# An MLP's up product taken before its norm, and two more of its pairs in seven products

## The reference, cut to what matters

```python
x = x + (merged @ w_out[l]).astype(x.dtype)
h2 = rmsnorm(x, norm_mlp_g[l])               # x * rsqrt(mean(x*x) + 1e-6) * g
z = jnp.square(jax.nn.relu(h2 @ w_up[l]))    # w_up: 1024 x 4096
x = x + (z @ w_down[l]).astype(x.dtype)      # w_down: 4096 x 1024
return rmsnorm(x, final_norm_g)              # then the second block begins with its own norm
```

## Time and profile before

| | us |
|---|---|
| median of 3 runs | 1552.71 (1552.62 to 1553.04) |
| profiled execution | 1552.45 |
| its span | 1550.7 |
| TensorE busy | 1540.2 |
| VectorE busy | 1059.2 |
| ScalarE busy | 755.2 |

### The profile page before, as it was taken

The page is one execution under the profiler, slowest core; times in us unless marked ns, Lnnn a source line. Parts: engine busy times, 40 slices in busy tenths (PEclk is TensorE's granted clock), DMA queues, the critical chain, the costliest instruction groups (busy, mean ns, idle before and its releaser), DMA issues.

```text
span 1550.7 us, 22343 instructions
## 1 busy us (share of the span) xinstructions
PE 1540.2 (99%) x8348; PEld 1326.7 (86%) x8348; DVE 1059.2 (68%) x1759; ACT 755.2 (49%) x1305; POOL 71.6 (5%) x62
## 2 busy tenths in 40 slices
PE   9999999999999999999999999999999999999998
PEld 7877777788799999888888888888888899989987
DVE  6776887668789576357786545455555899948735
ACT  5445776654357445264444334344444545524514
POOL 0000000020000000040000010020002000000002
PEclk9999999999999999999999999999999999999999
DMA  5333223242323332223442232334123333322322
GB/s 194 122 109 99 85 75 96 95 136 82 123 95 103 103 96 92 99 96 119 129 131 67 75 129 90 112 120 159 59 82 109 109 103 109 123 96 82 108 90 75
DMA packets 56235, 161.88 MB, mean 104 GB/s; under 512 B 7232, under 2 KB 8640, under 8 KB 56000
## 3 DMA queue, kind: packets, MB, share of 16 engines
q1 hardware_dynamic: 55504, 159.41, 31.9%
q0 software_dynamic: 320, 0.52, 0.2%
q10 hardware_dynamic: 304, 0.52, 0.1%
HBM read 148.89 MB, written 2.10 MB: 97 GB/s over the span
## 4 chain that ended last, share of the span: by engine, by line
PE 95%; DVE 4%; ACT 0%; issue 0%; DMA 0%; DVEq 0%; SPq 0%; ACTq 0%
PE G L1440 64%; PE TP L1440 10%; PE SC L1440 9%; PE O L1440 5%; PE M L1440 5%; DVE WL L2551 1%; PE TP L1874 1%; PE TP L1820 1%; DVE MGl L2551 0%; DVE T L2910 0%; DVE T L2914 0%; DMA GN<-in_gains 0%; PE TP L1923 0%; DVE QK L2551 0%; DVE F L3172 0%
## 5 line engine op out<-in xcount | busy, mean ns | idle before, releaser
L1440 PE MATMUL G<-XGh,WH 128*128 128x512 f32 x920 | 363.7, 395 | 0.0
L2551 DVE TENSOR_TENSOR WL<-RAW,WH 128x1024 fp32r<-128x1024 f32 (+2 forms) x269 | 282.9, 1056 | 115.8 <-ACT WH L1961 115.4
L1440 PE MATMUL G<-XGh,WL 128*128 128x512 f32 x920 | 358.7, 390 | 0.0
L1440 PE MATMUL G<-XGl,WH 128*128 128x512 f32 x920 | 358.3, 389 | 0.0
L1961 ACT ACTIVATE WH<-RAW 128x1024 fp32r<-128x1024 f32 (+2 forms) x275 | 240.1, 881 | 111.0 <-PE G L1440 79.8
L1440 PEld LDWEIGHTS G<-XGh,WH 128*128 128x128 f32 x920 | 172.8, 188 | 38.6 <-issue 3.8
L1440 PEld LDWEIGHTS G<-XGh,WL 128*128 128x128 f32 x920 | 172.7, 188 | 36.9
L1440 PEld LDWEIGHTS G<-XGl,WH 128*128 128x128 f32 x920 | 172.9, 188 | 33.9
L1440 PE MATMUL G<-MGl,WH 128*128 128x512 f32 x372 | 144.9, 389 | 1.0 <-DVE MGl L2551 1.0
L2902 DVE TENSOR_TENSOR X<-X,G 128x512 f32<-128x512 f32 x75 | 51.4, 686 | 137.2 <-PE G L1440 137.1
L1440 PE MATMUL G<-MGh,WH 128*128 128x512 f32 x372 | 145.0, 390 | 0.0
(11 more groups left out here) (423 smaller groups left out, 3226.3 us busy)
## 6 DMA issues: line engine op xcount, KB each, us to landing
RAW<-in_dn SPq DMA_DIRECT2D x30, 512.0 KB, 3.3
RAW<-in_fg SPq DMA_DIRECT2D x22, 512.0 KB, 4.3
RAW<-in_up SPq DMA_DIRECT2D x20, 512.0 KB, 3.4
RAW<-in_g SPq DMA_DIRECT2D x16, 512.0 KB, 3.3
RAW<-in_f SPq DMA_DIRECT2D x14, 512.0 KB, 3.7
X<-in_x SPq DMA_DIRECT2D x16, 256.0 KB, 4.3
RAW<-in_q SPq DMA_DIRECT2D x8, 512.0 KB, 3.3
RAW<-in_k SPq DMA_DIRECT2D x8, 512.0 KB, 3.3
```

The source lines that it names most:

```text
L1440: return e.matmul(dst, st, mv, start=start, stop=stop, skip_group_check=True)
L2551: return e.tensor_tensor(dst, src, hi.bitcast(F32), ALU.subtract)
```

## The change

The up product takes x*g without r. Its relu, its square and its high part are all ScalarE's now, and VectorE makes only the low part. VectorE's norm step makes r*r (ScalarE's Exp with -1.0, one refining step of two instructions) and leaves it in RB. "residual" of all 32 dn units multiplies the bank by RB into MSK (this frees the bank) and then adds MSK to X.

The sevens take XGh and XGl themselves as blocks, so the steps "h", "a_hi" and "a_lo" of the first section are gone; a new step "hx" on ScalarE writes x*g in float32 for the sums. `prepare_mid` starts this during `wo` 5. Units up 4 to 7 become pairs 2 and 3 of the sevens, and the order becomes up 0 to 3, pairs 2 to 7, dn 0 to 7, pairs 8 to 11, dn 8 to 15, pairs 12 to 15, dn 16 to 31. The second buffer of z is V in place of XG. Waits follow the tiles.

```diff
-MID, MID_FIRST, MID_PAIRS = 100, 4, 12
+MID, MID_FIRST, MID_PAIRS = 100, 2, 14
-    u += up(0) + down(0) + sevens(MID_FIRST, 12) + down(1) + sevens(12, 16) + down(2) + down(3)
+    u += up(0)[0:2 * MID_FIRST] + sevens(MID_FIRST, 8) + down(0) + sevens(8, 12) + down(1) + sevens(12, 16) + down(2) + down(3)
...
+            if n == 4:
+                self.prepare_mid(0)
...
+    def prepare_mid(self, start):
+
+        for kt in range(4):
+            for n, kinds in enumerate((("hx",), ("s13",), ("s2", "s4", "s_hi"), ("s_lo",))):
+                for kind in kinds:
+                    self.later(start + 3 * kt + n, kind, 0, kt)
...
         self.put("up", f)
+        self.put("up_sq", f)
         self.later(0, "up_hi", f)
         self.later(1, "up_lo", f)
...
-        self.prepare_sums(0, 1)
-        for f in range(1, 8):
+        for f in range(1, 2 * MID_FIRST):
             self.up(f)
             self.up_out(f)
-        self.down(0)
-        for p in range(MID_FIRST, 12):
-            self.seven_up(p)
-        self.down(1)
-        for p in range(12, 16):
-            self.seven_up(p)
-        self.down(2)
+        for q, (p0, p1) in enumerate(((MID_FIRST, 8), (8, 12), (12, 16))):
+            for p in range(p0, p1):
+                self.seven_up(p)
+            self.down(q)
         self.down(3)
...
+        ZP = (F[:, 2, :], MSK[:, :])
...
                     if name == "sums" and f == MID + MID_FIRST:
-                        e.wait_ge(r_done, NRM["norm", "mlp"])
-                    elif name == "sums" and f == MID + MID_FIRST + 1:
-                        e.wait_ge(prep_dve, PREP_DVE["s_lo", 0, 3])
+                        e.wait_ge(turned, TURN["turn_a", 7, 3])
...
                 elif kind == "mask_b":
                     e.wait_ge(sa_max, 2 * SA["scores_a", 7, 3])
-                    e.wait_ge(prep_dve, PREP_DVE["a_lo", 0, 3])
+                    e.wait_ge(dn_added, 32)
...
+                elif kind == "up":
+                    f = arg[0]
+                    if f == 1:
+                        e.wait_ge(r_done, NRM["norm", "mlp"])
+                    elif f >= 2:
+                        e.wait_ge(z_lo, UP[f - 2])
+                    e.wait_ge(unit_done, gemm_done(step))
+                    e.activation(ZP[f % 2], G[:, turn_of[step] % 2, :], ACT.Relu).then_inc(g_moved, 1)
+
+                elif kind == "up_sq":
+                    f = arg[0]
+                    e.wait_ge(g_moved, MOVED["up", f])
+                    e.activation(ZP[f % 2], ZP[f % 2], ACT.Square).then_inc(z_act, 1)
...
+                elif kind == "hx":
+                    section, kt = arg
+                    e.wait_ge(g_empty, EMPTY["residual", "wo", 4 + kt])
+                    if kt > 0:
+                        e.wait_ge(prep_dve, PREP_DVE["s4", 0, kt - 1])
+                    for at, k in zip(halves_of(0, kt), (kt, 4 + kt)):
+                        t = hi(at, X[:, k, :], gain(G_MLP, k))
+                    t.then_inc(prep_act, 1)
...
+            def refine_square(ms, r, tmp):
+
+                n_root[0] += 1
+                e.wait_ge(r_exp, n_root[0])
+                e.scalar_tensor_tensor(tmp, ms, -1.0, r, ALU.mult, ALU.mult).then_inc(r_sq, 2)
+                e.wait_ge(r_sq, 2 * n_root[0])
+                e.scalar_tensor_tensor(r, tmp, 2.0, r, ALU.add, ALU.mult).then_inc(r_done, 1)
...
                     bank = G[:, turn_of[step] % 2, :] if step in turn_of else SC[:, 0, :]
+                    if name == "dn":
+                        if i == 0:
+                            e.wait_ge(r_done, NRM["norm", "mlp"])
+                        else:
+                            e.wait_ge(dn_added, ADDED_DN[i - 1])
+                        e.tensor_tensor(SCALED_G, bank, R2, ALU.mult).then_inc(g_empty, 1)
+                        e.wait_ge(g_empty, EMPTY[step])
+                        e.tensor_tensor(X[:, n, :], X[:, n, :], SCALED_G, ALU.add).then_inc(dn_added, 1)
+                        continue
                     e.tensor_tensor(X[:, n, :], X[:, n, :], bank, ALU.add).then_inc(g_empty, 1)
-
-                elif kind == "up":
-                    f = arg[0]
-                    tt, z = T[:, f % 2, :], T[:, 2 + f % 2, :]
-                    if f == 0:
-                        e.wait_ge(r_done, NRM["norm", "mlp"])
-                    e.wait_ge(unit_done, gemm_done(step))
-                    e.tensor_tensor(tt, G[:, turn_of[step] % 2, :], RB[:, :], ALU.mult).then_inc(g_empty, 1)
-                    if f >= 2:
-                        e.wait_ge(z_hi, UP[f - 2])
-                    e.wait_ge(g_empty, EMPTY[step])
-                    e.scalar_tensor_tensor(z, tt, 0.0, tt, ALU.max, ALU.mult).then_inc(z_done, 1)
```

More of the change, by code:

```diff
@@ L218, in seven_loads @@
         behind = self.pair_held[side]
[L219 to L222, removed]
+        new = [("sums", key, None, max(behind, self.plain_held[3]) if side == 0 else behind),
+               ("b22", key, None, max(behind, self.plain_held[2])),
+               ("pair", key, side, max(behind, self.plain_held[side]))]
+        self.loads += new
         self.count[side] += 1
@@ L660, in down, with prepare_sums @@
                 self.put("xsplit", 2, n)
-    def prepare_sums(self, section, start):
+    def prepare_sums(self, start):
         for kt in range(4):
@@ L666, in prepare_sums @@
                 for kind in kinds:
-                    self.later(start + 5 * kt + n, kind, section, kt)
+                    self.later(start + 5 * kt + n, kind, 1, kt)
+    def prepare_mid(self, start):
[3 more added lines that the diff above has]
+                    self.later(start + 3 * kt + n, kind, 0, kt)
     def up_out(self, f):
         self.put("up", f)
+        self.put("up_sq", f)
         self.later(0, "up_hi", f)
@@ L1137, in program @@
         g_empty = sem("g_empty")
-        EMPTY = tally("qk", "residual", "up", "qk_b", "conv_g", "conv_y", "branch", "km", "qm", "fg", "fu", "fu_out",
+        EMPTY = tally("qk", "residual", "qk_b", "conv_g", "conv_y", "branch", "km", "qm", "fg", "fu", "fu_out",
                       "res_half")
         g_moved = sem("g_moved")
-        MOVED = tally("gate", "pool_in", "conv_u", "gate_b")
+        MOVED = tally("gate", "pool_in", "conv_u", "gate_b", "up")
+        dn_added = sem("dn_added")
+        ADDED_DN = {step[2]: n for step, n in tally("residual", but=[s for s in steps if s[:2] != ("residual", "dn")]).items()}
         half_gain, xn_mul, xn_hi, xn_lo = sem("half_gain"), sem("xn_mul"), sem("xn_hi"), sem("xn_lo")
@@ L1251, in program @@
             "prep_act", "prep_dve", "seven_act", "seven_dve", "t_sum"))
-        PREP_ACT, PREP_DVE = tally("s_hi", "a_hi"), tally("h", "s13", "s2", "s4", "s_lo", "a_lo")
+        PREP_ACT, PREP_DVE = tally("hx", "s_hi", "a_hi"), tally("h", "s13", "s2", "s4", "s_lo", "a_lo")
         SEVEN_ACT, SEVEN_DVE = tally("one_out", "c11", "silu"), tally("w_less", "v_less", "c22", "c12", "c21")
@@ L1560, in pv_heads, with left_of @@
                 return t
[L1562 to L1565, removed]
+            def left_of(j, kt, blocks):
+                if j in (0, 1, 3, 5):
+                    s = (0, 1, 3, 5).index(j)
+                    return SVh[s][:, kt, :], SVl[s][:, kt, :]
+                h, l = blocks
+                k, half = kt if j == 2 else 4 + kt, slice(HALF_S, S) if j == 6 else slice(0, HALF_S)
+                return h[:, k, half], l[:, k, half]
             for step in steps:
@@ L2258, in _ @@
                     n = 2 * (f - MID) + w
-                    if w == 1 and n % 8 == 1:
-                        e.wait_ge(unit_done, {9: unit("up", 7), 17: unit("dn", 7), 25: unit("dn", 15)}[n])
+                    if n == 9:
+                        e.wait_ge(pv_done, PV["pv_a", 7])
+                        e.wait_ge(sum_done, SUM["norm", "mlp"])
+                    elif n in (17, 25):
+                        e.wait_ge(unit_done, unit("dn", n - 10))
                     e.wait_ge(z_act, Z_ACT["square_b" if w else "square_a", f])
@@ L3137, in _ @@
                         e.wait_ge(*lo_made)
+                    elif i == 1 and section == 1:
+                        e.wait_ge(prep_dve, PREP_DVE["a_lo", 1, 2])
                     elif i == 1:
-                        e.wait_ge(prep_dve, PREP_DVE["a_lo", section, 2])
+                        e.wait_ge(sq_lo, SQH["acc_hi", "mlp"])
+                        e.wait_ge(r_done, NRM["norm", "mlp"])
                     if i == 0:
```

112 lines of the change are left out of this document (66 added, 46 removed).

## The result

The changed kernel takes **1564.48 us** (median of 6 runs, 1563.83 to 1565.21), the kernel before 1552.70 on the same chip (1552.27 to 1553.17): a ratio of 1.0075, 95% interval 1.0064 to 1.0086. That is 0.75% slower, twice what was forecast (+11.8 us for +5.8), and above the forecast's range. The profiled execution took 1563.83 with a span of 1562.0, 11.3 us over the span before.

What follows compares the result with a forecast made beforehand. TensorE, busy 99% of the span, was taken to bound the kernel. Terms -1.6 - 1.35 + 4.0 + 4.8 = +5.85 us on the profiled 1552.45 gave 1558.3, median 1558.5 us; range 1553.0 to 1562.0.

Steps and rivals of the forecast that it cites:

- what TensorE's work costs: Up product: two pairs in sevens at 10.08 us each replace plain units of 5.44 us, saving 1.6 us.
- The 1.2 us a pair: Sevens against plain units: saving estimated from the skill page's 6 + N cycles; the rows showed 0.8 us a pair.
- The -1.35 us at dn 0: At dn 0: TensorE's wait for z 7 goes, since six pairs now lie between up 3 and dn 0.
- The ring of 6.34 us: Residuals of dn 24 to 31: each turn grows from 5.60 to 6.34 us, making norm2 4.8 us late.
- the path behind r*r: First section of sevens: 8.2 us from r*r to up 1's relu, then about 12.9 us to the first one_out.
- What is late at the start of the sevens: Up 3 and the first pair: TensorE waits for up 1's relu and the first one_out, +4.0 us in total.
- At nothing: Items priced at zero, among them "hx" and s-steps in wo, said to fill 3.25 us of ScalarE idle time.
- the clock falls at norm2: Rival: half clock after TensorE's wait at norm2 adds 1.5 to 4 us, giving 1560 to 1562.5; chance 0.13.
- the one_out wait: First pair of sevens: TensorE's fifth product waits about 1.4 us for ScalarE's first one_out.
- Covered: Rival: other engines' idle time hides all added work, only -2.95 us is left, 1549.8 us; chance 0.13.

Runs made afterwards that it cites:

- e11: Changed kernel with twelve pairs, low part behind the residual in dn 24 to 31, sums from up 1, three steps apart: 1551.52 us, ratio 0.9992.
- e5: Kernel before, with only the residual of dn 24 to 31 made a multiply and then an add: 1559.87 us, ratio 1.0046.
- e2: Changed kernel, with the low part of the next weights put behind the residual in dn 24 to 31: 1558.06 us, ratio 1.0034.
- e13: As e11, but the sums begin during wo 5, as in the change: 1554.36 us, ratio 1.0011.
- e10: Changed kernel with twelve pairs and sums from up 1, five steps apart, low part ahead of the residual as in the change: 1569.30 us, ratio 1.0105.
- e7: Changed kernel with both edits of e2 and e3 together: 1557.90 us, ratio 1.0034.
- e4: Changed kernel, with the sums begun two units later in wo and two steps apart: 1573.25 us, ratio 1.0132.
- e3: Changed kernel, with the sevens' weights not split ahead during up 0 and up 1: 1563.64 us, ratio 1.0071.

## Why the prediction was right and wrong

**Right: what TensorE's work costs.** Both prices stood again: a pair in sevens took 10.08 us in the eight pairs after dn 0, a plain unit 5.44, so two pairs save 1.6 us. The 1.2 us a pair that the prediction worked out from the Trainium skill ("VectorE: DVE Perf Modes", TRN2 errata) does not hold here. The -1.35 us at dn 0 came, and e11 shows it as a gain in the end.

**Right: the residual of dn.** The ring of 6.34 us measured 6.33, in the change and in e5; norm2 began 4.3 us late for 4.8. e2 shows the reason was the given one: VectorE's fixed order around ScalarE's steps.

**Right: the path behind r*r.** The steps from r*r to the relu of up 1 measured, as a whole, 8.16 us for 8.2, and from there to one_out 12.97 for 12.9.

**The step that failed: "What is late at the start of the sevens", by where it starts.** It counted the lateness of wo 5 to 7 as at most 0.6 us for r*r (361.8 or 362.4); r*r was done at 365.7. The error stands in "At nothing": "hx and s-steps in wo fill idle time of 3.25 us on ScalarE". That idle time is a wait inside a ring, residual, XGh, XGl, low part of the weights, next residual. Before the change this ring had 0.97 us to spare in each unit (the row at 351.26: VectorE waits for TensorE). The sums went in front of the next residual and took more than that: the distances of the residuals rose from 5.44 to 5.99, 7.52 and 5.97. The 7.52 holds an add of 1.52 us beside GpSimd's, of a size that I had priced at 0.42, and a crossing to ScalarE and back (1.13 idle). e13 against e11 shows this cause alone. It gave the 2.15 us between up 0 and up 1, for which no term stood. Counted from up 1's late start, r*r was another 0.7 us later than forecast, and the unchanged 8.16 us behind it carried this to up 3: 3.55 for at most 2.9. In all the start cost 7.85 us for 4.0.

**The second part that failed: the clock was a rival and not a term.** I gave "the clock falls at norm2" 0.13 because my gap was "hardly longer" than 3.8 us, and did not ask it of the early wait at all. It fell behind both. At norm2 it cost 1.7 us on top of the wait, 6.0 for 4.8; e5 and e10 fell there too, each with a wait of over 4 us. At the start its 1.75 us stood mostly in the place of the one_out wait, forecast at 1.4: one_out came when the forecast had it, counted from the relu, and TensorE only asked later. In e7, where the clock did not fall, TensorE waits 2.1 us for it. So the early miss is r*r's. Taken off alone, the clock's 1.7 at norm2 leaves the median at 1562.8, above the range; the start's excess of 3.85 alone brings it inside, to 1560.6.

**The rivals.** "The clock falls at norm2" was right in its mechanism, with 1.7 us in its 1.5 to 4. "Covered" (1549.8) was not reached by any kernel with 14 pairs; e11, with twelve, is at 1551.5, and two more pairs without a wait would take 1.6 off that, an estimate.

## What to carry to other kernels

Idle time of an engine between two steps of a ring is not free room: before putting work there, ask how much the ring has to spare against the engine that sets the pace, if the work lands in front of the ring's next step, and if it can go behind it instead (e2: 6.4 us for one instruction moved behind two). When products are moved forward, all that must be prepared for them moves too; count its queue steps in the new order (a plain unit two, a seven one) and not in the old one. And a stall on TensorE is priced with the half clock that may follow it, here 1.5 us (e10) to 3.0 (e4) around waits of 3.4 to 4.2, unless another engine is the one that TensorE would wait for next.

## What the runs showed of the hardware

- In the change a VectorE add of 128x256 took 1.52 us where a GpSimd add ran beside it (343.55 beside 343.44 to 344.78) and 0.42 otherwise: 1.1 us more, most of GpSimd's 1.34. The Trainium skill's "GPSIMD Engine Reference" says in its table, under SBUF interfaces, that VectorE's instructions with two SBUF inputs contend with GpSimd; the trace agrees.
- The same wait did not always cost the same. Behind 3.38 and 3.36 us (the change, e2) the following unit took 7.19 and 8.21 us; behind a one_out wait of 2.1 us the clock fell in e3 and not in e7; it fell within the 4.15 us wait in e5, and only at the end of the 4.16 us in the change (1.00 over 700 to 706). The Trainium skill ("TensorE: Matmul & The Clock Gate", part 1) has the clock watched by a monitor that isn't in step with the kernel; these traces are in keeping with that, but show no monitor. The spreads differ too: 2.7 us over six runs of e7 and 2.1 over five of e2, 0.9 over 11 of e11, but also 0.6 over four of e5.
